# Last two experts' rows of the gate's first two tiles placed by weighted one-hot products; two output row buffers; scaling of a tile split over two engines

## The reference, cut to what matters

```python
def hier_moe(x, ...):                       # 16 experts in 4 groups, 2 chosen per token
    ...                                     # group by argmax, top 2 of its 4 experts
    top_w = softmax(top_vals) * g_w[:, None]
    hgu = einsum("td,edf->tef", xt, w_gate_up)
    gate, up = split(hgu, 2, axis=-1)
    a = silu(gate) * up * combine[:, :, None]
    return einsum("tef,efd->td", a, w_down)
# per layer
x = layer_norm(ALPHA * x + mixer(x), ln1_g[i], ln1_b[i])
x = layer_norm(ALPHA * x + hier_moe(x), ln2_g[i], ln2_b[i])
gate = sigmoid(einsum("bsd,de->bse", x, ple_w_gate[i]) + ple_b_gate[i])
x = x + gate * einsum("bsp,pd->bsd", p[i], ple_w_proj[i])
```

## Time and profile before

| | us |
|---|---|
| median of 3 runs | 1387.23 (1382.13 to 1390.22) |
| the profiled execution: its time, its span | 1381.82, 1380.3 |
| PE busy | 1269.5 (92%) |
| DVE busy | 817.8 (59%) |
| ACT busy | 568.1 (41%) |
| POOL busy | 213.5 (15%) |
| the experts of layer 0, first gate and up product to last output copy | 603.41 to 773.44 |
| the same of layer 1 | 1119.42 to 1286.40 |

### The profile page before, as it was taken

The page is one execution under the profiler, slowest core; times in us unless marked ns, Lnnn a source line. Parts: engine busy times, 40 slices in busy tenths (PEclk is TensorE's granted clock), DMA queues, the critical chain, the costliest instruction groups (busy, mean ns, idle before and its releaser), DMA issues.

```text
span 1380.3 us, 21295 instructions
## 1 busy us (share of the span) xinstructions
PE 1269.5 (92%) x8445; PEld 1183.7 (86%) x8445; DVE 817.8 (59%) x1149; ACT 568.1 (41%) x624; POOL 213.5 (15%) x217
## 2 busy tenths in 40 slices
PE   5999999999999999989999389999999989999288
PEld 5999999999999998877777289999998878877288
DVE  4643444453635544678888676445435678888673
ACT  4323223122131213267888444121213268878441
POOL 2210011000100003422232000000004422221000
PEclk9999999999999999999999689999999899999689
DMA  9453334242423203169999733221203169999501
GB/s 293 140 182 107 116 122 121 78 142 73 149 74 111 95 27 125 54 234 355 366 358 373 248 123 94 65 92 62 77 28 115 54 256 368 375 378 355 201 1 69
DMA packets 93044, 229.59 MB, mean 166 GB/s; under 512 B 9574, under 2 KB 56846, under 8 KB 80560
## 3 DMA queue, kind: packets, MB, share of 16 engines
q1 hardware_dynamic: 74640, 179.84, 37.0%
q0 software_dynamic: 18336, 48.79, 10.3%
HBM read 209.90 MB, written 33.37 MB: 176 GB/s over the span
## 4 chain that ended last, share of the span: by engine, by line
PE 69%; DMA 19%; DVE 5%; ACT 4%; issue 3%; POOLq 0%; DVEq 0%; SPq 0%; ACTq 0%
PE ps L1512 19%; PE ps L1513 18%; PE ps L1514 18%; DMA y_scratch<-expert_y,slot_row 16%; ACT expert_y L830 2%; PE ps L1600 2%; PE ps L1663 1%; PE ps L1664 1%; PE ps L1665 1%; DVE w_lo L993 1%; PE ps L1801 1%; DMA w_raw<-in_a_w_in 1%; PE ps L1802 1%; DVE xT L1382 1%; PE ps L1803 1%
## 5 line engine op out<-in xcount | busy, mean ns | idle before, releaser
L993 DVE TENSOR_TENSOR w_lo<-w_raw,w_hi 128x2048 fp32r<-128x2048 f32 (+1 forms) x164 | 359.2, 2209 | 99.6 <-ACT w_hi L704 98.6
L704 ACT ACTIVATE w_hi<-w_raw 128x2048 fp32r<-128x2048 f32 (+1 forms) x164 | 299.6, 1851 | 89.1 <-PE ps L1514 75.3
L1512 PE MATMUL ps<-x_hi,w_hi 128*128 128x288 f32 (+2 forms) x1024 | 306.6, 299 | 12.5 <-DVE x_lo L1388 12.0
L1514 PE MATMUL ps<-x_hi,w_lo 128*128 128x288 f32 (+2 forms) x1024 | 304.1, 297 | 0.0
L1513 PE MATMUL ps<-x_lo,w_hi 128*128 128x288 f32 (+2 forms) x1024 | 304.1, 297 | 0.0
L1512 PEld LDWEIGHTS ps<-x_hi,w_hi 128*128 128x128 f32 x1024 | 195.1, 191 | 15.1 <-issue 12.7
L1513 PEld LDWEIGHTS ps<-x_lo,w_hi 128*128 128x128 f32 x1024 | 195.2, 191 | 0.0
L1514 PEld LDWEIGHTS ps<-x_hi,w_lo 128*128 128x128 f32 x1024 | 195.1, 191 | 0.0
L1512 PE MATMUL ps<-w_hi,x_hi 128*128 128x256 f32 x480 | 137.4, 286 | 4.0 <-DVE v_stage L1033 4.0
L1513 PE MATMUL ps<-w_lo,x_hi 128*128 128x256 f32 x480 | 136.9, 285 | 0.0
L1514 PE MATMUL ps<-w_hi,x_lo 128*128 128x256 f32 x480 | 136.9, 285 | 0.0
(11 more groups left out here) (260 smaller groups left out, 2142.6 us busy)
## 6 DMA issues: line engine op xcount, KB each, us to landing
w_raw<-in_moe_w_gate_up SPq DMA_DIRECT2D x64, 1024.0 KB, 7.3
w_raw<-in_moe_w_down SPq DMA_DIRECT2D x32, 1024.0 KB, 8.2
w_raw<-in_a_w_in SPq DMA_DIRECT2D x24, 1024.0 KB, 5.3
w_raw<-in_a_w_out SPq DMA_DIRECT2D x12, 1024.0 KB, 5.1
w_raw<-in_b_w_in SPq DMA_DIRECT2D x12, 1024.0 KB, 5.2
w_raw<-in_ple_w_gate SPq DMA_DIRECT2D x8, 1024.0 KB, 8.0
w_raw<-y_scratch SPq DMA_DIRECT2D x8, 1024.0 KB, 8.3
v_scratch<-v_stage POOLq DMA_DIRECT2D x12, 512.0 KB, 3.5
```

The costliest lines, as they stand in the source:

```text
L704: act.activation(whi[:, j, 0:n], raw[:, j, 0:n], ACT.Copy).then_inc(hi_done, 1)
L993: dve.tensor_tensor(wlo[:, j, 0:n], raw[:, j, 0:n], whi[:, j, 0:n].bitcast(f32), ALU.subtract).then_inc(split_done, 1)
L1512: pe.matmul(out, sh, mh, start=first, stop=False)
L1514: ins = pe.matmul(out, sl, mh, start=False, stop=final)
```

## The change

1. **Two output buffers.** `expert_y` has two halves, used by turns; `y_out(s)` waits for the scatter of s-2 in place of that of s-1. The one semaphore `y_st` becomes two.
2. **The last two experts (14 and 15) for token tiles 0 and 1.** Their rows of these tiles no longer go through DRAM. DVE makes, for each of the two experts and tiles, a 128x128 float32 one-hot matrix times the slot's weight (`last_onehot`, four instructions before step 14). PE multiplies it with the expert's output (`last_rows(n)`, 4 float32 matmuls of 512 columns for each expert) into PSUM banks 6, 7, 2, 3. DVE adds the sum from PSUM (`add_last`). Their other rows are scattered with a second list, `row_late`, that leaves out tokens under 256. So that the load of tiles 0 and 1 finds zeros there, POOL scatters zero rows for experts 14 and 15 at step 4. To have each slot's weight, POOL stores the 1152 weights in DRAM, 4 bytes each, and gathers those of the two experts back.
3. **Loads of rows.** Tile 0 is loaded when the scatter of expert 13 has landed, tile 1 right behind it into the gather buffer; tiles 2 to 4 when all scatters have.
4. **The hand-over rewritten.** For tiles 0 and 1 DVE does the normalisation in one instruction; of their scaling DVE does 4 columns and ACT 4; for tiles 2 to 4 ACT does all 8. Tiles 2 to 4 are added after the splits of tiles 0 and 1. A square root of a constant comes first on ACT, so that the table for it is loaded then. `hi` and `lo` of the last two gate weight units move behind the first tiles.
5. **Small ones.** DVE copies the ranks and computes `last_at` and `row_late` before the first expert (6 instructions). The branch for an expert with more than 128 tokens uses other buffers; no expert takes it in this trace.

```diff
@@ scatter, POOL
+                pool.memset(zero[:, :], 0.0)
+                ch.link(pool.memset(w_slot[:, :], 0.0))
...
                 for s in range(4, NE):
                     gather(s)
                     expert_rows(s - 4)
+                    if s == 4:
+                        for n in range(2):
+                            pool.indirect_dma_start(out=y_dram[l][:, :], out_offset=bass.IndirectOffsetOnAxis(ap=row_idx[:, NE - 2 + n:NE - 1 + n], axis=0),
+                                                    in_=zero[:, :], in_offset=None, bounds_check=2 * T - 1, oob_is_err=False).then_inc(side_st, 16)
+                        pool.wait_ge(w_ok, l + 1)
+                        w_rows = w_dram[l].rearrange("(k t) o -> k (t o)", k=2)
+                        for k in range(2):
+                            pool.dma_start(w_rows[k, 0:TP].rearrange("(i p) -> p i", p=P), wtop[:, k, 0:4], allow_slow_non_contiguous=True).then_inc(side_st, 16)
+                            pool.dma_start(w_rows[k, TP:T].rearrange("(p o) -> p o", o=1), wtop[0:TS, k, 4:5]).then_inc(side_st, 16)
@@ y_out, ACT
                     act.wait_ge(eu_used, it * (3 * step) + (EU * l + dn_unit(s) + 1))
-                    if l or s or step:
-                        act.wait_ge(y_st, q * 16)
-                    act.activation(y_sb[:, :].rearrange("p (b t) -> p b t", b=2), ps[:, 4:6, :], ACT.Copy).then_inc(y_cp, 1)
+                    if l or s >= 2 or step:
+                        act.wait_ge(y_st[s % 2], it * (8 * step) + 16 * ((NE // 2) * l + s // 2))
...
+                    act.activation(y_sb[:, s % 2, :].rearrange("p (b t) -> p b t", b=2), ps[:, 4:6, :], ACT.Copy).then_inc(y_cp, 1)
@@ the end of the experts, PE
+                def last_rows(n):
+                    pe.wait_ge(ohw_ok, l + 1)
+                    for i in range(2):
+                        for h in range(2):
+                            pe.wait_ge(yl_ok if n and h == 0 else y_cp, l + 1 if n and h == 0 else NE * (l + 1) - 1 + n)
+                            ins = pe.matmul(ps[:, LAST_BANK[i] + h, :], ohw[:, n, i, :], y_sb[:, n, 512 * h:512 * h + 512], start=(n == 0), stop=(n == 1))
...
-                for s in range(NE - 2, NE + 1):
+                for s in range(NE - 2, NE):
                     moe_step(s)
+                last_rows(0)
+                moe_step(NE)
...
+                last_rows(1)
@@ the loads of rows, SP
+                for par in range(2):
+                    sp.wait_ge(y_st[par], 16 * (NE // 2 * (l + 1) - 1))
+                sp.wait_ge(side_st, 96 * (l + 1))
+                sp.wait_ge(split_done, U_G[l] + 1)
+                rows_load(0)
+                sp.wait_ge(xtp, 2 * NE * (l + 1))
+                rows_load(1)
```

More of the change, by code:

```diff
@@ L91, in trunk @@
     y_dram = [nc.dram_tensor(f"y_scratch{l}", (2 * T, D), f32).ap() for l in range(DEPTH)]
+    w_dram = [nc.dram_tensor(f"w_scratch{l}", (2 * T, 1), f32).ap() for l in range(DEPTH)]
     y_prompt = outs[0][0].rearrange("(i p) d -> p i d", p=P)
@@ L269, in trunk @@
         xg_ld = [sem("x_gathered0"), sem("x_gathered1")]
-        yg_ld = [sem(f"y_gathered{j}") for j in range(4)]
+        yg_ld = [sem(f"y_rows_loaded{i}") for i in range(NT)]
         ov_ld, ovx_ld = [sem("ovf_w0"), sem("ovf_w1")], [sem("ovf_x0"), sem("ovf_x1")]
@@ L394, in trunk @@
         TR_IN = 0
-        TR_N2 = [NT, NT * 2]
+        TR_N2 = [NT + 1, NT * 2]
+        LAST_BANK = (6, 2)
         V_DONE = NT * VU
@@ L675, in _ @@
                     pool.wait_ge(xtp, 2 * NE * (l + 1))
-                    pool.wait_ge(y_st, 16 * NE * (l + 1))
+                    for par in range(2):
+                        pool.wait_ge(y_st[par], 16 * (NE // 2) * (l + 1))
                     pool.wait_ge(o["idxcopied"], 1)
@@ L917, in out_copy @@
                     act.activation(o_sb[0:tok(i), i, 512 * h:512 * h + 512], out_bank(u)[0:tok(i), :], ACT.Copy).then_inc(out_a, 1)
+                act.activation(warm[:, :], eps[:, :], ACT.Sqrt)
                 squares(0)
                 std_of(0)
-                norm(0)
                 squares(1)
                 std_of(1)
-                norm(1)
+                scale(0)
                 tile_hi(0)
+                scale(1)
+                tile_hi(1)
+                hi(U_G[l] + 3)
                 squares(2)
-                tile_hi(1)
                 std_of(2)
                 norm(2)
+                gate(0)
+                scale(2)
+                tile_hi(2)
+                gate(1)
                 squares(3)
+                squares(4)
                 std_of(3)
+                std_of(4)
                 norm(3)
-                tile_hi(2)
-                squares(4)
-                std_of(4)
                 norm(4)
-                gate(0)
-                gate(1)
+                gate(2)
+                scale(3)
                 tile_hi(3)
-                gate(2)
+                gate(3)
+                scale(4)
                 tile_hi(4)
-                for q in range(3, GQ):
+                for q in range(4, GQ):
                     gate(q)
@@ L1391, in tile_low @@
                 def tile_low(i):
+                    if i == 0:
+                        for par in range(2):
+                            dve.wait_ge(y_st[par], 16 * (NE // 2) * (l + 1))
                     x_low(i + 1, P * i, P * i + tok(i))
@@ L1417, in _ @@
                 tile_low(1)
+                add_rows(2, 0)
+                add_rows(2, 1)
+                lo(U_G[l] + 2)
                 rstd2(2)
+                add_rows(3, 0)
                 add_rows(3, 1)
+                gated(0)
                 add_rows(4, 0)
                 add_rows(4, 1)
+                tile_low(2)
+                lo(U_G[l] + 3)
+                gated(1)
                 rstd2(3)
-                scale2(2)
                 rstd2(4)
-                tile_low(2)
-                gated(0)
-                scale2(3)
-                gated(1)
+                gated(2)
                 tile_low(3)
-                scale2(4)
-                gated(2)
+                gated(3)
                 tile_low(4)
-                for q in range(3, GQ):
+                for q in range(4, GQ):
                     gated(q)
```

213 lines of the change are left out of this document (139 added, 74 removed).

## The result

| | before | changed |
|---|---|---|
| median (lowest to highest), us | 1384.73 (1382.13 to 1390.22) | 1406.32 (1402.87 to 1410.47) |
| the profiled execution's span | 1380.3 | 1401.1 |

The ratio is 1.0158, 95% interval 1.0128 to 1.0188: the changed kernel is slower by 21.6 us, where 8.1 less was forecast.

What follows compares the result with a forecast made beforehand. In the experts PE, DMA and the copy-scatter loop lie within 5% of each other; at the hand-over PE stands still. -6.5 + 5.2 - 6.8 = -8.1 us gave a median of 1379.1 us (chance 0.43), range 1366 to 1391.

Steps and rivals of the forecast that it cites:

- Part 2: Cost added in the experts: zero rows +3.2, small pieces +1, DVE's small instructions +1, in all +5.2 us.
- The upper bound: Small pieces in the experts: 1296 packets at POOL's mean 0.124 us on 16 engines, 10.0 us a layer; 0.5 was taken.
- Part 1: Experts, two output buffers: the copy no longer waits for the scatter; -6.5 us in all, bounds 0 and -12.8.
- rival C: Experts: DMA already sets the pace, two buffers give 0, side transfers cost 5.2, hand-over gain stays; 1385.6 us, chance 0.23.
- rival B: Experts: DMA gives way and PE sets the pace, two buffers give -12.8, zero rows hidden; 1368.6 us, chance 0.20.
- part 3: End of the experts: the scatter wait goes, the last rows' products come in; T stays, 0 within 1.5 us.
- T: Start of a layer's last output copy, at 772.4 us in layer 0 of the kernel before.
- Part 4: Hand-over behind the experts: first gate matmul at T+17.9, not T+28.6; gain 3.4 us a layer, -6.8 for both.
- D: Experts: pieces of 4 bytes are dear in the DMA stage, so slower; 1394.4 or 1404.6 us by price, chance 0.14.

## Why the prediction was wrong, step by step

**Part 2 failed, at one term.** It put the stores of 4 bytes at 0.5 us a layer, by the row of a 16 KB load that lands in 2.9 us. Copy 0 to copy 13 in the changed kernel and in the one with 40-byte pieces differ by 10.0 and 10.6 us. The row was the wrong neighbour: it is a read of DRAM, and the price is one of writes that lie side by side. The upper bound, 10.0 us a layer from the mean packet of POOL's queue, came out as the size, but that is luck. It counted 1296 packets a layer at 0.124 us, one for each piece; the stores add 128 packets a layer, 1.0 us by the same sum. The time stands in the others' rows, 21.77 us for a gather, 18.47 for a weight block, and the same 74640 packets of SP's queue at 8496 us in place of 8171. The sign named in that part, a gather waited for by PE, did show it (21.0 us, before 4.4).

The other terms of part 2: zero rows 3.2 forecast; copy 0 to copy 13 with the weights' way out is 5.6 us longer in sum than with two buffers alone, and 0.8 shorter when they are moved: 6.4, twice the forecast, and avoidable. Gathers of single weights and what belongs to them: 1.4 and 0.8 us. DVE's small instructions, 1 forecast: 0, copy 0 came no later.

**Part 1 was right in sign, and short in size for another reason than forecast.** -6.5 forecast with bounds 0 and -12.8; -9.4 by the ratio (6.8 to 12.2 less), alone. The forecast was a shorter step all through the experts, 9.9 and 10.0, and named a step that stays at 10.2 as a sign of being wrong. It stayed or nearly so: 10.1 and 10.2 in the two traces of the two buffers alone, 10.36 and 10.28 in the changed kernel. So the limit of rival C holds from copy 5 on (DMA share 1.00, waits for weights), and rival B, that PE would set the pace, falls. The gain inside the experts, some 3.5 us over both layers, lies ahead of copy 5, and half of the whole is at experts 14 and 15, which I had counted in part 3.

**Part 3 was right as stated and misread in worth.** T after copy 13 moved by -0.5 and +1.5 us, within the 1.5 given. With two buffers alone it comes 3.3 and 1.3 earlier: the products of the last rows take the place of that gain, as the text says, only that T does not matter then. In the new order the adds start from the load of rows behind scatter 13.

**Part 4 was right by its own count.** First gate matmul forecast at T+17.9, measured 18.1 and 18.3; PE before tile 3 forecast to stand 4.2 us, measured 5.04 and 4.9; the clock fell there (transposes of 1.94 us); the gain from T to tile 4 forecast as 2.8 with the fall, measured 2.9 and 2.7; the fifth gate tile came at T+42.2 and T+42.5, within the 40 to 42.5 given. The loads in it were taken too short: tile 0's rows were there at T+0.4 (layer 0), not T-1, and tile 1's at T+3.3 (layer 1), not T+2.5, although the scatter ahead of them landed 0.7 us earlier than forecast. But the part counted against the kernel with one buffer. Against two buffers it is 0, since the old order gains as much from the end of the wait. Why the new one can't do better is argued from the rows, not tested: in the 57.7 us from copy 13 to tile 4 ACT is busy 41.9 us where it was 33.1 with two buffers alone, DVE 41.6 where it was 41.2, and PE's idle time only moves behind the first gate matmul (1.61 and 5.04 us, for the norms of ACT).

```profile
753.80:811.30 57.50, 30.27 (x180) 26.92 (x178) 41.22 (x68) 33.12 (x38) 3.96 (x3) 0.76 0.64 220
```

```profile
767.60:825.30 57.70, 39.57 (x197) 31.60 (x195) 41.57 (x58) 41.87 (x65) 3.02 (x3) 0.85 0.60 203
```

(Two buffers alone above, the changed kernel below; columns as in the earlier trace rows.)

**The rivals and the range.** D named the right culprit, pieces of 4 bytes dear in that stage, but not how they cost; its upper price, 1404.6, is 1.7 us from the median by the luck told above. It had 0.14. The range ended at 1391, although a bound of 10.0 us a layer had been worked out from a row: the bound was written down and then left out. Against D stood one row of a transfer in the other direction, and that was too little.

## What to carry to other kernels

A store whose pieces are a few bytes and lie side by side in DRAM (here each from another partition, which was not varied) is to be costed by what it does to all other transfers. In this kernel that was 10 us a layer for 4.6 KB in the full stage, and still 7 to 8 us when they were issued earlier, where the DMA engines had time free. Lay the data out so that each partition writes its own run, or set the pieces apart. When one change holds several parts, cost each against the kernel with the others in it: here one part alone had all the gain, and another only gave a second time what the first had given. A gain at a hand-over is to be counted from an event that neither order moves, here the copy of expert 13, not from the last copy before it.

## What the runs showed of the hardware

- Side by side, 1152 stores of 4 bytes (4.6 KB) left 196 GB/s over 20 us at a DMA share of 0.91; with 64 bytes from one to the next 362 GB/s were moved in the same stretch. In the changed kernel it was 246 over 21 us, and 381 over 20 us with pieces of 40 bytes.
- The price shows in loads and gathers that are under way meanwhile: 21.77 us for a gather with a median of 9.5 before, 19.92 for a block of 1 MB in the kernel with the stores alone. A few packets carry it: 58 of 12288 took over 2.5 us there, none without the stores or with 64 bytes between the pieces, and the median stayed 0.309 us.
- The number of packets says nothing of the number of pieces: 2304 pieces of 4 bytes added 256 packets to POOL's queue.
- A load of 1 MB of rows from `y_scratch` right behind the scatter of expert 13 took 7.45 and 9.94 us in the two layers of the changed kernel, and 11.73 in layer 1 of the run with the products moved; the load on the chain of the kernel before, behind the last scatter, took 4.91.
